# Weight sums of the gated feed-forward stages: four GpSimd additions per weight slot become one preloaded block and three accumulating transfers

## What is computed

```python
FFN_HIDDEN = -(-8 * D_MODEL // (3 * 256)) * 256        # 2816
...
def swiglu(h, w_in, w_out):
    g, u = jnp.split(h @ w_in, 2, axis=-1)
    return (jax.nn.silu(g) * u) @ w_out
...
    h = h + swiglu(rms_norm(h, a_ffn_norm[i]), a_ffn_w_in[i], a_ffn_w_out[i])
...
    h = h + swiglu(rms_norm(h, b_ffn_norm[j]), b_ffn_w_in[j], b_ffn_w_out[j])
```

## Time and profile before

| | |
|---|---|
| median of three runs | 3287.18 us |
| the three runs | 3286.41, 3287.18, 3288.49 us |
| span of the profiled execution | 3286.2 us |
| PE busy in it | 3255.1 us (99%) |
| DVE, POOL, ACT busy | 2027.2, 1028.5, 730.0 us |
| moved by DMA | 304.51 MB, mean 93 GB/s |

### The profile page before, as it was taken

The page is one execution under the profiler, slowest core; times in us unless marked ns, Lnnn a source line. Parts: engine busy times, 40 slices in busy tenths (PEclk is TensorE's granted clock), DMA queues, the critical chain, the costliest instruction groups (busy, mean ns, idle before and its releaser), DMA issues. The chain is left out here.

```text
span 3286.2 us, 40354 instructions
## 1 busy us (share of the span) xinstructions
PE 3255.1 (99%) x15522; PEld 2464.8 (75%) x15522; DVE 2027.2 (62%) x3686; ACT 730.0 (22%) x1567; POOL 1028.5 (31%) x806
## 2 busy tenths in 40 slices
PE   8999999999999999999999999999999999999999
PEld 6767775555555566788888854888886887888888
DVE  8766777676765624278545656756536688866543
ACT  3432422010101333131111124211101235321111
POOL 0111323323232010224444401444441453344443
PEclk9999999999999999999999999999999999999999
DMA  6434412333331121332222221222223221122222
GB/s 261 138 102 128 126 52 79 114 122 110 119 107 55 61 88 49 97 87 78 90 90 90 80 87 64 80 88 90 90 90 101 81 82 53 40 77 90 90 90 90
DMA packets 66896, 304.51 MB, mean 93 GB/s; under 512 B 8496, under 2 KB 21168, under 8 KB 40720
## 3 DMA queue, kind: packets, MB, share of 16 engines
q1 hardware_dynamic: 54368, 268.68, 24.3%
q0 software_dynamic: 6528, 18.75, 1.8%
q10 hardware_dynamic: 5808, 14.49, 1.3%
HBM read 292.84 MB, written 2.88 MB: 90 GB/s over the span
## 5 line engine op out<-in xcount | busy, mean ns | idle before, releaser
L2857 POOL TENSOR_TENSOR scratch<-ring 128x512 f32<-128x512 f32 (+1 forms) x160 | 217.1, 1357 | 1443.6 <-PE psum L744 952.9
L744 PE MATMUL psum<-big,scratch 128*128 128x256 f32 (+1 forms) x2240 | 606.9, 426 | 0.0
L744 PEld LDWEIGHTS psum<-big,scratch 128*128 128x128 f32 x2240 | 425.6, 190 | 163.7
L744 PE MATMUL psum<-H,scratch 128*128 128x256 f32 (+1 forms) x2144 | 498.9, 387 | 0.0
L744 PEld LDWEIGHTS psum<-H,scratch 128*128 128x128 f32 x2144 | 406.5, 190 | 77.0 <-issue 5.0
L744 PE MATMUL psum<-big,ring 128*128 128x256 f32 (+1 forms) x1584 | 421.4, 418 | 6.6 <-DVE cb L2172 2.5
L744 PE MATMUL psum<-H,ring 128*128 128x256 f32 (+1 forms) x1536 | 396.2, 400 | 1.7 <-issue 0.7
L744 PEld LDWEIGHTS psum<-big,ring 128*128 128x128 f32 x1584 | 300.1, 190 | 111.9 <-DVE cb L2172 3.7
L1480 ACT ACTIVATE cb<-psum 128x256 f32<-128x256 f32 x336 | 129.0, 384 | 1011.0 <-PE psum L744 1011.0
L744 PEld LDWEIGHTS psum<-H,ring 128*128 128x128 f32 x1536 | 290.0, 190 | 76.8 <-ACT H L1578 6.4
L713 PE MATMUL psum<-H,ring 128*128 128x512 f32 x736 | 328.6, 598 | 0.0
(11 more groups left out here) (397 smaller groups left out, 4144.6 us busy)
## 6 DMA issues: line engine op xcount, KB each, us to landing
ring<-in_wall SPq DMA_DIRECT2D x202, 1024.0 KB, 4.9
big<-in_wada SPq DMA_DIRECT2D x48, 512.0 KB, 3.5
big<-in_wada POOLq DMA_DIRECT2D x32, 512.0 KB, 4.1
big<-in_wada SPq DMA_DIRECT2D x8, 1024.0 KB, 21.1
scratch<-in_rpb ACTq DMA_DIRECT2D x16, 512.0 KB, 4.0
big<-big ACTq DMA_DIRECT2D x64, 64.0 KB, 4.9
X<-in_xin SPq DMA_DIRECT2D x4, 768.0 KB, 6.9
scratch<-negd SPq DMA_DIRECT2D x8, 384.0 KB, 9.1
```

The costliest lines, as they stand in the source:

```text
L744: mm = pe.matmul(fast_bank(st, q, b), lhsT, rhs(k), start=start and k == 0, stop=k == kt - 1, skip_group_check=True)
L2857: pool.tensor_tensor(s1, a21, a22, ALU.add).then_inc(combo_own, 1)
```

## The change

In the stages of `PLUS` (SW0 and SW1) POOL adds nothing any more. The host lays the weights out differently: of each slot, `wall` holds the three blocks a22, a11, a12 (768 KB for SP to load), and a new array `wsum` holds the 1 MB block (a21, a11, a21, a12), which SP loads straight into `combos` once product 7 of slot q-2 is done. Then POOL issues three transfers that add what they read to what they write: first a22 and a11 onto positions 0 and 2 (s1 = a21 + a22 and a21 + a11), then position 0 onto position 1 (a11 + s1), then position 1 onto position 3 (a12 + a11 + s1). Each waits for the one before it, and the next slot's first waits for this slot's last. The signs that turn a difference into a sum are put on the activations and on the products; three DVE operations per slot or pair change from a plain tensor operation to one with a scalar (-1.0), and ACT copies product 5 with the scale -1.0.

```diff
+PLUS = [SW0, SW1]
+PLUS_SLOTS = [st.slot0 + x for st in PLUS for x in range(len(st.slots()))]
...
-                sp.dma_start(ring[:, r * SLOT:(r + 1) * SLOT], wall[n]).then_inc(arrived[r], 16)
+                w = 1536 if n in PLUS_SLOTS else SLOT
+                sp.dma_start(ring[:, r * SLOT:r * SLOT + w], wall[n][:, 0:w]).then_inc(arrived[r], 16)
+                if n in PLUS_SLOTS:
+                    q = FAST[n]
+                    sp.wait_ge(prod[7], q - 1)
+                    sp.dma_start(combos[q % 2].rearrange("p i k c -> p (i k c)"), wsum[PLUS_SLOTS.index(n)])\
+                      .then_inc(sum_begun[q % 2], 16)
...
-                    act.activation(piece(st, p, q), fast_bank(st, q, b), ACT.Copy).then_inc(copied[i], 1)
+                    act.activation(piece(st, p, q), fast_bank(st, q, b), ACT.Copy, scale=-1.0 if st in PLUS and i == 5 else 1.0)\
+                       .then_inc(copied[i], 1)
...
-                    dve.tensor_tensor(shaped(st, h_mix(st, i, j)), a, b, ALU.subtract).then_inc(mixed_ready, 1)
+                    out = shaped(st, h_mix(st, i, j))
+                    if st not in PLUS or i == 2:
+                        ins = dve.tensor_tensor(out, a, b, ALU.subtract)
+                    elif i == 0:
+                        ins = dve.tensor_tensor(out, b, a, ALU.subtract)
+                    else:
+                        ins = dve.scalar_tensor_tensor(out, b, -1.0, a, ALU.mult, ALU.subtract)
+                    ins.then_inc(mixed_ready, 1)
...
-                        own(dve.tensor_tensor(t[0], l12, l11, ALU.subtract))
+                        own(dve.tensor_tensor(t[0], l11, l12, ALU.subtract))
...
-                        dve.tensor_tensor(t[1], hB, t[0], ALU.subtract).then_inc(hid_mid, 1)
+                        dve.scalar_tensor_tensor(t[1], t[0], -1.0, hB, ALU.mult, ALU.subtract).then_inc(hid_mid, 1)
...
-                    dve.tensor_tensor(hA, fast_bank(st, q, 1), gA, ALU.mult).then_inc(c21_done, 1)
+                    dve.scalar_tensor_tensor(hA, fast_bank(st, q, 1), -1.0, gA, ALU.mult, ALU.mult).then_inc(c21_done, 1)
...
+            def add_weights(st):
+                nonlocal sums
+                for x, (kind, g, s) in enumerate(st.slots()):
+                    q, slot = st.q0 + x, st.slot0 + x
+                    r, n = slot % RING, st.k_half(kind, g) * P
+                    a = ring[:, r * SLOT:(r + 1) * SLOT].rearrange("p (b c) -> p b c", b=4)
+                    c = combos[q % 2].rearrange("p i k c -> p i (k c)")
+                    pool.wait_ge(combos_ready, q)
+                    pool.wait_ge(arrived[r], 16 * (slot // RING + 1))
+                    pool.wait_ge(sum_begun[q % 2], BEGUN_FROM + 16 * (sum(FAST[m] % 2 == q % 2 for m in PLUS_SLOTS if m <= slot)))
+                    sums += 1
+                    pool.dma_start(c[:, 0:4:2, 0:n], a[:, 0:2, 0:n], accum_op=ALU.add).then_inc(sum_two, 16)
+                    pool.wait_ge(sum_two, SUMS_FROM[0] + 16 * sums)
+                    pool.dma_start(c[:, 1, 0:n], c[:, 0, 0:n], accum_op=ALU.add).then_inc(sum_three, 16)
+                    pool.wait_ge(sum_three, SUMS_FROM[1] + 16 * sums)
+                    pool.dma_start(c[:, 3, 0:n], c[:, 1, 0:n], accum_op=ALU.add).then_inc(sum_four, 16)
+                    pool.wait_ge(sum_four, SUMS_FROM[2] + 16 * sums)
+                    pool.sem_inc(combos_ready, 1)
...
-            mix_weights(SW0)
+            add_weights(SW0)
...
-            mix_weights(SW1)
+            add_weights(SW1)
```

More of the change, by code:

```diff
@@ L158, in wait, with build @@
             self.eng.wait_ge(self.sem, self.n)
[L161 removed]
+def build(nc, xin, wall, wsum, wada, cvec, wgate, wlru, vec, bgate, con, mask2, rpb, pos, out, negd):
     with ExitStack() as ctx:
@@ L293, in build @@
         first_in = [sem(f"first_in{g}") for g in range(4)]
-        mod_in = [[sem(f"mod_in{q}_{r}") for r in range((MOD_RING, 4)[q])] for q in range(2)]
+        mod_and_sum_in = [[sem(f"modulation_and_sum_in{q}_{r}") for r in range((MOD_RING, 4)[q])] for q in range(2)]
+        mod_in = mod_and_sum_in
+        sum_two, sum_three, sum_four = mod_and_sum_in[0]
+        sum_begun = mod_and_sum_in[1][0:2]
+        SUMS_FROM, BEGUN_FROM = (11 * 16, 11 * 16, 10 * 16), 12 * 16
         mod_used = sem("mod_used")
@@ L741, in product @@
                             ready(k, kt)
-                        lhsT = combos[q % 2][:, cols, k, :] if cols < 4 else \
-                            slot_cols(r, (cols - 4) // 2 * kt + k, (cols - 4) % 2 * P, P)
+                        if cols < 4:
+                            lhsT = combos[q % 2][:, cols, k, :]
+                        elif st in PLUS:
+                            at = r * SLOT + {4: 512, 6: 1024, 7: 0}[cols] + k * P
+                            lhsT = ring[:, at:at + P]
+                        else:
+                            lhsT = slot_cols(r, (cols - 4) // 2 * kt + k, (cols - 4) % 2 * P, P)
                         mm = pe.matmul(fast_bank(st, q, b), lhsT, rhs(k), start=start and k == 0, stop=k == kt - 1,
@@ L2152, in relu2, with third_output @@
                     step(dve.scalar_tensor_tensor(x, x, 0.0, x, ALU.max, ALU.mult))
+                def third_output(st, i, out, product, copy):
+                    if st in PLUS and i == 7:
+                        return dve.tensor_tensor(out, copy, product, ALU.subtract)
+                    return dve.tensor_tensor(out, product, copy, ALU.add)
                 def took(i, q, done, out, also):
@@ L2158, in took @@
                     dve.wait_ge(copied[also], q + 1)
-                    dve.tensor_tensor(piece(st, p, q) if out is None else out, fast_bank(st, q, b), piece(st, p, q), ALU.add)\
-                       .then_inc(done, 1)
+                    third_output(st, i, piece(st, p, q) if out is None else out, fast_bank(st, q, b), piece(st, p, q))\
+                        .then_inc(done, 1)
                     dve.wait_ge(done, q + 1)
@@ L2171, in to_residual @@
                         if i == 7:
-                            dve.tensor_tensor(c, fast_bank(st, q, b), c, ALU.add).then_inc(done, 1)
+                            third_output(st, i, c, fast_bank(st, q, b), c).then_inc(done, 1)
                             dve.wait_ge(done, q + 1)
@@ L2183, in to_residual @@
                     dve.wait_ge(prod[4], q + 1)
-                    to_x(2 * s + 1, 0, fast_bank(st, q, 1)).then_inc(c21_done, 1)
+                    if st in PLUS:
+                        x = x_half(st, 2 * s + 1, 0)
+                        dve.tensor_tensor(x, x, fast_bank(st, q, 1), ALU.subtract).then_inc(c21_done, 1)
+                    else:
+                        to_x(2 * s + 1, 0, fast_bank(st, q, 1)).then_inc(c21_done, 1)
                     if last:
@@ L2864, in mix_weights @@
                     after(x)
+            sums = 0
+            def add_weights(st):
[16 more added lines that the diff above has]
+                    pool.sem_inc(combos_ready, 1)
             pool.wait_ge(scaled_done, 6)
@@ L3068, in _layout @@
     assert wall.shape[0] == N_SLOTS, wall.shape
+    wsum = np.zeros((len(PLUS_SLOTS), P, 4, 4, P), np.float32)
+    for i, (st, x) in enumerate((st, x) for st in PLUS for x in range(len(st.slots()))):
+        kt = st.k_half(*st.slots()[x][0:2])
+        a = wall[st.slot0 + x].reshape(P, 8, 2, P).copy()
+        a11, a12, a21, a22 = a[:, 0:kt, 0], a[:, kt:2 * kt, 0], a[:, 0:kt, 1], a[:, kt:2 * kt, 1]
+        for b, part in enumerate((a21, a11, a21, a12)):
+            wsum[i, :, b, 0:kt] = part
+        blocks = np.zeros((P, 4, 4, P), np.float32)
+        for b, part in enumerate((a22, a11, a12)):
+            blocks[:, b, 0:kt] = part
+        wall[st.slot0 + x] = blocks.reshape(P, SLOT)
     vecs = {"final_g": f["final_g"], "a_norm": f["a_norm_2"],
@@ L3084, in _layout @@
         "wall": wall,
+        "wsum": wsum.reshape(len(PLUS_SLOTS), P, SLOT),
         "wada": np.ascontiguousarray(wada),
```

2 lines of the change are left out of this document (1 added, 1 removed).

## The result

The changed kernel takes **3601.71 us** (median of 4 runs, 3590.95 to 3603.03) against 3286.97 us before (the three runs above and one more): a ratio of 1.095, 95% interval 1.0934 to 1.0965. That is 315 us slower than before and 192 us above the top of the range. The profiled execution took 3602.47 us, with a span of 3600.6 us.

The account below looks back on a forecast made before the run. PE, working without a gap, was taken as the bound. Sums late only in short slots add 7.4 us to the profiled 3286.2, giving 3293.6; the runs' median lies 1.0 higher, so 3294.6 us; range 3285 to 3410 us.

Parts of the forecast that it names:

- What bounds the kernel: In SW0 and SW1 PE works without a gap; nothing POOL, DVE or the queues do faster gives back over 1.1 us.
- What is removed: POOL's 272 additions, off PE's path, and with them a brake on DVE's two-SBUF-tensor operations; worth at most about 1.1 us.
- DVE and ACT: Operations with a scalar -1.0 and the scaled copy, costed at nothing; without cover, 0.1 us per slot would be 7 us.
- SP's queue: The added 1 MB load per slot does not hold up the ring loads and lands in 4.9 us.
- What is added on POOL: Three accumulating transfers in a row, bounded at 9.5 to 13.9 us in full slots, 8.3 to 11.7 us in short ones.
- the middle value: The time taken for the three transfers between both bounds: 11.7 us in full slots, 10.0 us in short ones.
- traffic beside it leads to much the same: Claim that other traffic gives 13.8 us for the three transfers, much like the 13.9 us from a second operand.
- the sum: Full slots: load 4.9 plus transfers 11.7 is 16.6 us, under the 16.95 us available; short slots lose 7.4 us in all.
- Rival 2: POOL becomes the bound once the three transfers exceed 12.08 us; at 13.9 us, 123 us lost, 3410 us; chance 0.35.
- Rival 1: The accumulating transfers cost no more than plain copies, 9.5 and 8.3 us: no change, 3288.4 us; chance 0.20.
- Rival 3: PE gets faster because POOL leaves SBUF alone; 6.6 us would need 1.8 ns off each record's 215.8 ns; chance 0.03.
- The signs named in advance: Readings to tell the cases apart: transfer landings, PE's idle places, POOL's start distances (12.1 us or longer), DVE's line 2244 towards 0.43 us.

## Why the prediction was wrong

- **What bounds the kernel: right.** PE without a gap, nothing to gain but about 1.1 us; the kernel without the sums is at 1.0000.
- **What is removed, DVE and ACT, SP's queue: right in price.** No sums, and POOL's additions in the new layout, cost nothing measurable. The ring load behind SP's new load landed in 4.2 us there.
- **What is added on POOL: this step failed.** It took 11.7 us for the three, with 13.9 as the upper end; the slot shows 17.1 in the mean and 17.35 in the one taken apart above. The adding by itself was not the error: the minima are 4.4, 3.0 and 2.9 us, and the medians without the block load 5.0, 3.3 and 3.9, 12.2 us. Two other things were. *The hand-overs* were put at nothing: a transfer's landing is not the next one's issue, and after the third POOL signals, waits for its own signal and only then issues. The slot without the block load is 13.84 us for 12.2 us of landings, 1.6 us. With them the middle value would have been 13.3 us, above the 12.08 us. *The company of the loads* was taken as another way to the same upper end: "traffic beside it leads to much the same", 13.8 us, in place of the second operand and not on top of it. The runs show both at once. The block load's company is 2.7 us of the slot in the mean; with the 12.2 and the 1.6 us, and half a microsecond for the longer slots that are there without the load too, that is some 17 us. For the block load itself the text looked at 6.9 us; it measured 5.6. SP's load is released by product 7, and with PE late that stands just ahead of the third transfer (2173.90 and 2177.04 in the slot above).
- **Forecast and rivals.** The full slots had 0.35 us to spare by the sum, less than either term that was missing. Rival 2's mechanism came true with its point of decision: no pause on POOL, gaps before product 5 in every slot, PE at POOL's pace above 12.08 us. Its price was taken from 13.9 us. With 17.1 us a slot, the mean over SW0's 23 distances, its own sum gives 28 x 5.0 = 140 us per stage for the full slots, 280 us for both, and the short ones add to it. What spoke against it, that the average load stays below what the engines can do, was true only just: a share of 0.69 at 17.1 us is 11.7 us of the engines in a slot that should take 12.08. It was also beside the point: the chain waits for one transfer at a time, and that transfer for whatever is out beside it.
- **Rival 1** had plain copies hidden or nearly so, 3288.4 us. Plain copies beside the block load gave 3356.31 us, without it 3289.79 us: its price held only for transfers left alone. The Trainium skill (DMA: Bandwidth & Descriptors, section "Anatomy of one DMA — SWDGE (gpsimd) path") gives 3.2 us for 512 KB by its formula; the plain copies' median is 3.2 us, so the trace agrees there, and not for accumulating ones, with 5.0 us. The estimate that the prediction took from it, some 8.4 us for the three with nothing late, is far from the slot of 17.1 us that the changed kernel shows.
- **Rival 3:** no record of PE came closer than before. PE's busy time rose.
- **The signs named in advance** told it at once: the starts of line 2915 are some 17 us apart, and PE's idle time is put down to POOL's signal 68 times, as often as the two stages have slots, not in the last slots alone. DVE's line 2244 (now 2279) fell to 0.42 us, as was said for every case.

## What to carry to other kernels

A chain of dependent transfers that repeats must fit into the period with its hand-overs and with the loads that its own consumer releases, not with landings read in quiet stretches: put the issue times of the other queue beside the chain, as they will stand once the consumer is late. An add inside a transfer took 2.2 times the DMA engines' time of a copy, so it belongs where those engines have that time free, not beside a load of the same size in a period that is full. Two reasons for the same higher price, here the second operand and the traffic beside it, are added unless a row shows that they exclude each other. When the sum leaves less to spare than one hand-over, the case behind the threshold is the likelier one.

## What the runs showed that was not expected

- **A small transfer beside loads pays for them, not for itself:** 64 KB landed in 5.6 us in the median, with a minimum of 2.3 us; 256 KB in the same place took 6.5 us.
- **DVE's slow operations come from coincidence with POOL's, not from POOL's additions as such.** The earlier trace rows has 1485 ns for line 2244. In the kernel before it runs beside POOL's last addition of a slot:

```profile
3006.95 1.33 POOL L2862 TENSOR_TENSOR scratch<-ring,scratch 128x512 f32<-128x512 f32 x1
3007.07 1.49 DVE L2244 TENSOR_TENSOR big<-big 128x256 f32<-128x256 f32 x1
```

 In the kernel with POOL's additions in the new layout, POOL still adds in every slot, but only once the block load has landed, and the 22 executions of the same operation (line 2279) take 418 ns in the mean. The timeline of that kernel, POOL's last addition of a slot and DVE's operations after it:

```profile
3005.32 1.26 POOL L2920 TENSOR_TENSOR scratch<-scratch 128x512 f32<-128x512 f32 x1
...
3010.67 0.43 DVE L2278 TENSOR_TENSOR big<-big 128x256 f32<-128x256 f32 x1
3011.01 0.42 DVE L2279 TENSOR_TENSOR big<-big 128x256 f32<-128x256 f32 x1
```

 Where POOL's additions still meet DVE's work on two SBUF tensors in that kernel, as at the start of a stage (line 2079), single executions take up to 1486 ns there too. The prediction named the right brake, but it goes with a shift of POOL's work in time as well as with its removal. Neither moved the kernel's time.
- **PE's fall to the 1.2 GHz level** after waits near 5 us (432 ns a record) stands behind the 100.8 of the 313 us by which PE was busy longer in the trace, and with the clock back at 0.98 the time was 5 us lower, less than the runs of one kernel differ. What an account by busy time makes a third of the loss was no cause of it.
